# Time mixer of a hybrid decoder block: low-rank products and the three sums by ones as f32r products of split operands, in new instruction orders

## The reference, cut to what matters

```python
r, k, v, wl, al, gl = jnp.split(pf, cuts, axis=-1)          # 3 x 2048, 96, 96, 256
decay = jnp.exp(-DECAY_SCALE * jax.nn.sigmoid(w0 + jnp.tanh(wl) @ w_w2))
a = jax.nn.sigmoid(a0 + al @ w_a2)
g = jax.nn.sigmoid(gl) @ w_g2
kk = heads(k * k_k); kk = kk / jnp.maximum(jnp.linalg.norm(kk, axis=-1, keepdims=True), 1e-12)
k = k * (1.0 + (a - 1.0) * k_a)
y = rwkv7_scan(r_h, w_h, k_h, v_h, kk, a_h)                 # state S (64 x 64) per head, token after token
y = ((y - ym) * lax.rsqrt(yv + GN_EPS)) * gn_g + gn_b       # mean and variance over a head
bonus = jnp.sum(r_h * k_h * r_k, axis=-1, keepdims=True) * v_h
y = (y + bonus) * g
```

## Time and profile before

| what | value |
|---|---|
| median of the runs | 2427.96 us |
| the profiled execution | 2426.78 us, its span 2424.9 us |
| busy over the span | TensorE 2151.6 us (89%), VectorE 1532.0 (63%), ScalarE 676.7 (28%), GpSimd 668.7 (28%) |
| granted TensorE clock | 0.989 of full speed on the mean |
| software DMA queue (expert rows) | 537.01 MB, 52.7% of the 16 engines' span |
| VectorE, `w_half_rest` L192 | 224 instructions, 1218 ns each |
| ScalarE, `w_half_high` L171 | 224 instructions, 1051 ns each |

### The profile page before, as it was taken

The page is one execution under the profiler, slowest core; times in us unless marked ns, Lnnn a source line. Parts: engine busy times, 40 slices in busy tenths (PEclk is TensorE's granted clock), DMA queues, the critical chain, the costliest instruction groups (busy, mean ns, idle before and its releaser), DMA issues.

```text
span 2424.9 us, 37735 instructions
## 1 busy us (share of the span) xinstructions
PE 2151.6 (89%) x15287; PEld 1506.1 (62%) x15287; DVE 1532.0 (63%) x2592; ACT 676.7 (28%) x1353; POOL 668.7 (28%) x538
## 2 busy tenths in 40 slices
PE   7999999999999999998988988978887787777776
PEld 6999999999899999886544444433332233222222
DVE  7778888888765545558765577667445544444445
ACT  4555555555344444433111111111111000000000
POOL 1000000000000000004554555555455545444542
PEclk9999999999999999999999999999999999999999
DMA  5433333333366666677999999999999999999997
GB/s 201 131 105 101 104 89 96 102 89 100 106 188 192 186 185 188 198 249 276 416 416 424 421 426 427 427 426 427 427 427 427 426 427 427 428 427 427 427 427 289
DMA packets 346272, 708.19 MB, mean 292 GB/s; under 512 B 13834, under 2 KB 270434, under 8 KB 279778
## 3 DMA queue, kind: packets, MB, share of 16 engines
q0 software_dynamic: 74176, 537.01, 52.7%
q1 hardware_dynamic: 271684, 168.55, 23.5%
q10 hardware_dynamic: 240, 0.22, 0.0%
HBM read 703.63 MB, written 2.10 MB: 291 GB/s over the span
## 4 chain that ended last, share of the span: by engine, by line
DMA 33%; PE 15%; DVE 2%; issue 2%; POOL 1%; DVEq 1%; ACT 0%; POOLq 0%; ACTq 0%
DMA down_rows<-in_v_table,experts 25%; DMA up_rows<-in_u_table,experts 8%; PE bank L1782 8%; PE project L1782 4%; PE bank L1698 2%; POOL down_rows L1686 1%; DVE up_rows L1898 0%; PE bank L1740 0%; PE bank L1746 0%; PE bank L1725 0%; ACT diagonal L1842 0%; DVE one_hot L1348 0%; PE bank L1714 0%; DVE expert_sides L1354 0%; PE bank L1708 0%
## 5 line engine op out<-in xcount | busy, mean ns | idle before, releaser
L1898 DVE CUSTOM_DVE_ANT_0 up_rows<-up_rows,h 128x2048 f32<-128x2048 f32 x256 | 585.1, 2291 | 525.8 <-DMA up_rows<-in_u_table,experts 525.8
L1782 PE MATMUL bank<-down_rows,diagonal 128*128 128x512 f32 x1520 | 709.3, 603 | 144.5 <-DMA down_rows<-in_v_table,experts 112.0
L1782 PEld LDWEIGHTS bank<-down_rows,diagonal 128*128 128x128 f32 x1520 | 281.3, 191 | 554.4 <-issue 310.5
L1680 POOL DMA_INDIRECT up_rows<-in_u_table,experts x256 | 291.4, 1138 | 1159.2 <-POOLq L1366 1048.1
L1686 POOL DMA_INDIRECT down_rows<-in_v_table,experts x256 | 369.0, 1442 | 524.2 <-PE bank L1782 510.6
L192 DVE TENSOR_TENSOR w_half_rest<-w_half,w_half_high 128x1024 fp32r<-128x1024 f32 x224 | 271.3, 1218 | 160.1 <-ACT w_half_high L171 159.9
L207 PE MATMUL project<-hT_high,w_half_high 128*128 128x272 f32 (+1 forms) x1152 | 351.2, 305 | 0.4 <-PEq L214 0.3
L207 PE MATMUL project<-hT,w_half_high 128*128 128x272 f32 (+1 forms) x1152 | 329.3, 286 | 0.0
L207 PE MATMUL project<-hT_high,w_half_rest 128*128 128x272 f32 (+1 forms) x1152 | 328.8, 285 | 0.0
L1782 PE MATMUL project<-down_rows,diagonal 128*128 128x512 f32 x512 | 259.1, 630 | 71.2 <-DMA down_rows<-in_v_table,experts 65.8
L171 ACT CAST w_half_high<-w_half 128x1024 fp32r<-128x1024 f32 x224 | 234.8, 1051 | 205.4 <-PE merge_ps L207 121.0
(11 more groups left out here) (376 smaller groups left out, 3035.3 us busy)
## 6 DMA issues: line engine op xcount, KB each, us to landing
w_half<-in_w_in SPq DMA_DIRECT2D x176, 512.0 KB, 4.0
w_half<-in_w_branch_a SPq DMA_DIRECT2D x32, 512.0 KB, 3.7
out_w<-in_w_out SPq DMA_DIRECT2D x16, 1024.0 KB, 6.3
query_w<-in_w_q_peer SPq DMA_DIRECT2D x10, 1024.0 KB, 30.4
w_half<-in_w_branch_b SPq DMA_DIRECT2D x16, 512.0 KB, 3.7
out_w<-in_w_q_peer SPq DMA_DIRECT2D x6, 1024.0 KB
up_rows<-in_u_table,experts POOLq DMA_INDIRECT x256, 21.1
down_rows<-in_v_table,experts POOLq DMA_INDIRECT x256
```

The lines of the kernel that those rows point to most:

```text
L1680: pool.indirect_dma_start(ur[n % RU], None, w["u_table"][0], bass.IndirectOffsetOnAxis(ap=k.idx[:, t, h, j:j + 1], axis=0)).then_inc(s_u[n ...
L1782: mm = nc.tensor.matmul(acc[t][c][:], dg[n % RD][:], vr[n % RV][:, quarter(c)], start=(n == 0), stop=(n == last(t, c)), skip_group_check=True)
L1898: v.tensor_tensor_reduce(ur[n % RU], ur[n % RU], k.h[:, n // (HEADS * TOPK), :], 1.0, 0.0, ALU.mult, ALU.add, dots[:, n:n + 1]).then_inc(s ...
```

## The change

- The low-rank weights of a pair (four parts of 128 columns) go into one tile `w2` of 128x512, split by ScalarE (rounding) and VectorE (rest) in a new unit `lr`; the low-rank inputs are split once, at pair 0. Decay, rate and gate products then are three f32r products each (two times three for the gate).
- The squares of kk, the squares of y and r·k·r_k are split too: the squares are written twice by ScalarE, once rounded; r·k is rounded by ScalarE in a new unit `rq`. VectorE makes the rests in new units `nq`, `rq`, `gq`. The ones are exact in f32r, so each sum is two f32r products.
- k's rate factor (`k_scale`) moves from VectorE to ScalarE, behind the tanh of the rate.
- The three lists are new. SyncE loads a pair's low-rank weights when the split of the pair before has been made.
- The new tiles lie over tiles that are not yet in use (parts of `ya_high`, `ya_rest`, `pool_in`) or over the tile that they are made from.

```diff
 PE_ORDER = (
-    ("t", 1, 2), ("rb", 0, 2), ("u", 0, 3), ("lw", 0, 1), ("f", 10, 0), ("s", 0, 3), ("Z", 1, 2), ("r", 1, 3), ("la", 0, 1),
-    ("f", 3, 0), ("T", 1, 2), ("u", 1, 3), ("lg", 0, 1), ("f", 3, 0), ("s", 1, 3), ("r", 2, 3), ("T", 2, 2), ("u", 2, 3),
-    ("nm", 0, 1), ("f", 6, 0), ("s", 2, 3), ("r", 3, 3), ("T", 3, 2), ("u", 3, 3), ("f", 8, 0), ("s", 3, 3), ("r", 4, 3),
-    ("T", 4, 2), ("u", 4, 3), ("bo", 0, 1), ("f", 8, 0), ("s", 4, 3), ("Z", 5, 2), ("t", 0, 1), ("gv", 0, 3), ("f", 10, 0),
-    ("T", 5, 2), ("gr", 0, 1), ("r", 0, 2),
+    ("gr", 0, 2), ("t", 1, 2), ("u", 0, 3), ("f", 3, 0), ("lw", 0, 1), ("f", 2, 0), ("s", 0, 3), ("Z", 1, 2), ("rb", 0, 2),
+    ("r", 1, 3), ("f", 2, 0), ("la", 0, 1), ("f", 2, 0), ("lg", 0, 1), ("f", 6, 0), ("u", 1, 3), ("T", 1, 2), ("f", 3, 0),
+    ("s", 1, 3), ("r", 2, 3), ("T", 2, 2), ("u", 2, 3), ("f", 3, 0), ("s", 2, 3), ("r", 3, 3), ("T", 3, 2), ("u", 3, 3),
+    ("f", 2, 0), ("nm", 0, 1), ("f", 3, 0), ("s", 3, 3), ("r", 4, 3), ("T", 4, 2), ("f", 6, 0), ("bo", 0, 1), ("f", 5, 0),
+    ("Z", 5, 2), ("u", 4, 3), ("t", 0, 1), ("s", 4, 3), ("f", 4, 0), ("gv", 0, 3), ("f", 7, 0), ("r", 0, 2), ("T", 5, 2),
 )
 ACT_ORDER = (
-    ("sq", 0, 1), ("ge", 0, 4), ("lg", 0, 1), ("r", 2, 3), ("kn", 0, 1), ("e", 0, 0), ("ex", 0, 1), ("split", 4, 0),
-    ("u", 2, 3), ("nm", 0, 1), ("r", 3, 3), ("u", 3, 3), ("r", 4, 3), ("split", 5, 0), ("split", 0, -1), ("e", 1, 0),
-    ("u", 4, 3), ("yc", 0, 3), ("yf", 0, 2), ("gv", 0, 3), ("split", 1, -1), ("t", 0, 1), ("t", 1, 1), ("r", 0, 2), ("e", 2, 0),
-    ("u", 0, 2), ("lo", 0, 1), ("split", 2, -1), ("lw", 0, 0), ("la", 0, 0), ("r", 1, 2), ("ab", 0, 0), ("split", 3, -1),
-    ("u", 1, 2),
+    ("u", 0, 3), ("lo", 0, 2), ("lw", 0, 1), ("split", 2, 0), ("la", 0, 1), ("r", 1, 3), ("kn", 0, 1), ("split", 3, 0),
+    ("u", 1, 3), ("ex", 0, 1), ("r", 2, 3), ("e", 0, 0), ("rq", 0, 1), ("ge", 0, 4), ("u", 2, 3), ("sq", 0, 1), ("split", 4, 0),
+    ("r", 3, 3), ("u", 3, 3), ("lg", 0, 1), ("nm", 0, 1), ("ab", 0, 1), ("split", 5, 0), ("e", 1, 0), ("split", 0, -1),
+    ("yf", 0, 2), ("r", 4, 3), ("u", 4, 3), ("lr", 0, 0), ("yc", 0, 3), ("gv", 0, 3), ("r", 0, 2), ("e", 2, 0), ("t", 0, 1),
+    ("split", 1, -1), ("t", 1, 1),
 )
 DVE_ORDER = (
-    ("ge", 0, 4), ("split", 2, 0), ("go", 0, 4), ("s", 0, 3), ("e", 2, 1), ("rb", 0, 2), ("Z", 1, 2), ("r", 1, 3), ("la", 0, 1),
-    ("T", 1, 2), ("gy", 0, 4), ("s", 1, 3), ("cv", 0, 0), ("lk", 0, 1), ("split", 3, 0), ("T", 2, 2), ("r", 2, 3), ("s", 2, 3),
-    ("e", 0, 0), ("r", 3, 3), ("ks", 0, 1), ("T", 3, 2), ("split", 4, 0), ("s", 3, 3), ("nr", 0, 1), ("T", 4, 2), ("bo", 0, 1),
-    ("kb", 0, 1), ("rs", 0, 1), ("split", 5, 0), ("split", 0, -1), ("e", 1, 0), ("Z", 5, 2), ("split", 1, -1), ("T", 5, 2),
-    ("gr", 0, 1), ("Z", 0, 1), ("gm", 0, 1),
+    ("split", 5, 1), ("gq", 0, 4), ("split", 0, 0), ("lr", 0, 1), ("Z", 5, 3), ("ge", 0, 4), ("T", 5, 3), ("gr", 0, 2),
+    ("Z", 0, 2), ("split", 1, 0), ("gm", 0, 2), ("rs", 0, 2), ("s", 0, 3), ("Z", 1, 2), ("cv", 0, 0), ("rb", 0, 2),
+    ("la", 0, 1), ("e", 2, 1), ("split", 2, 0), ("go", 0, 4), ("r", 1, 3), ("lk", 0, 1), ("T", 1, 2), ("s", 1, 3),
+    ("split", 3, 0), ("T", 2, 2), ("r", 2, 3), ("s", 2, 3), ("gy", 0, 4), ("nq", 0, 1), ("split", 4, 0), ("r", 3, 3),
+    ("ks", 0, 1), ("T", 3, 2), ("s", 3, 3), ("e", 0, 0), ("rq", 0, 1), ("nr", 0, 1), ("T", 4, 2), ("bo", 0, 1), ("kb", 0, 1),
+    ("e", 1, 0),
 )
...
@block.sync
+                if b == 0:
+                    sp.wait_ge(q["zero"], n_zero)
-                wait(sp, q["lora_mm"], b * 3)
+                wait(sp, q["w2_split"], b)
...
@block.tensor
+            def low_rank(i, n, out, t0, start=True, stop=True):
+                return product(nc, out, [x[0:n, i, :] for x in (w2_high, w2_rest)], [x[0:n, i, t0:T] for x in (lora_high, lora_rest)], start, stop)
+            def by_ones(out, high, rest):
+                nc.tensor.matmul(out, ones_r[:].bitcast(F32R), high.bitcast(F32R), start=True, stop=False)
+                return nc.tensor.matmul(out, ones_r[:].bitcast(F32R), rest.bitcast(F32R), start=False, stop=True)
             def lw(_, p, par):
-                wait(pe, q["lora_w"], p * 48 + 48)
+                wait(pe, q["w2_split"], p + 1)
...
-                nc.tensor.matmul(low[:, 0:T], ww2[:], k.lora[0:DECAY_LORA, 0, :], start=True, stop=True).then_inc(q["lora_mm"], 1)
+                low_rank(0, DECAY_LORA, low[:, 0:T], 0).then_inc(q["lora_mm"], 1)
...
             def nm(_, p, par):
-                nc.tensor.matmul(low[:, 0:T], ones, sq[:, real], start=True, stop=True).then_inc(q["norm"], 1)
+                by_ones(low[:, 0:T], sq_high[:], sq_rest[:]).then_inc(q["norm"], 1)
...
@block.scalar
             def sq_(_, p, par):
+                nc.scalar.activation(sq_high[:].bitcast(F32R), kx[par][:, real], ACT.Square, scale=cur[par][:, V_KK:V_KK + 1])
+                nc.scalar.activation(sq[:], kx[par][:, real], ACT.Square, scale=cur[par][:, V_KK:V_KK + 1]).then_inc(q["ksq"], 1)
+            def lr(_, p, par):
+                if p == 0:
+                    for i, (_, c) in enumerate(k.lora_tiles):
+                        nc.scalar.copy(lora_high[0:c, i, :].bitcast(F32R), k.lora[0:c, i, :]).then_inc(q["lora_high"], 1)
+                wait(act, q["lora_mm"], p * 3)
+                wait(act, q["lora_w"], p * 48 + 48)
+                nc.scalar.copy(w2_high.bitcast(F32R), w2[:]).then_inc(q["w2_high"], 1)
+            def rq(_, p, par):
+                wait(act, q["bonus"], p)
+                wait(act, q["rk"], p + 1)
+                nc.scalar.copy(rk_high.bitcast(F32R), rk[:]).then_inc(q["rkhigh"], 1)
             def la(_, p, par):
...
+                act.wait_ge(q["sig"], p * 3 + 2)
+                nc.scalar.activation(t1[:, real], am[:, real], ACT.Identity, scale=cur[par][:, V_KAH:V_KAH + 1],
+                                     bias=cur[par][:, V_KAC:V_KAC + 1]).then_inc(q["kscale"], 1)
             def y(_, p, par):
+                nc.scalar.activation(ysq_high.bitcast(F32R), y_ps, ACT.Square)
...
@block.vector
             def la(_, p, par):
-                wait(dve, q["sig"], p * 3 + 2)
-                n.tensor_scalar(t1[:, real], am[:, real], cur[par][:, V_KAH:V_KAH + 1], cur[par][:, V_KAC:V_KAC + 1], ALU.mult, ALU.add)
             def lk(_, p, par):
+                wait(dve, q["kscale"], p + 1)
+            def lr(_, p, par):
+                if p == 0:
+                    n.tensor_copy(ones_r[:].bitcast(F32R), ones).then_inc(q["ones"], 1)
+                    for i, (_, c) in enumerate(k.lora_tiles):
+                        dve.wait_ge(q["lora_high"], i + 1)
+                        rest_bits(n, lora_rest[0:c, i, :], k.lora[0:c, i, :], lora_high[0:c, i, :])
+                wait(dve, q["w2_high"], p + 1)
+                rest_bits(n, w2_rest, w2[:], w2_high).then_inc(q["w2_split"], 1)
+            def nq(_, p, par):
+                rest_bits(n, sq_rest[:], sq[:], sq_high[:]).then_inc(q["ksplit"], 1)
+            def rq(_, p, par):
+                rest_bits(n, rk_rest[:], rk[:], rk_high).then_inc(q["rksplit"], 1)
+            def gq(_, p, par):
+                rest_bits(n, ysq_rest[:], ysq[:], ysq_high).then_inc(q["sqsplit"], 1)
```

More of the change, by code:

```diff
@@ L688, in lg @@
                 for j in range(2):
-                    mm = nc.tensor.matmul(low[:, 0:SEQ], wg2[:, j, :], k.lora[:, 2 + j, META:T], start=(j == 0), stop=(j == 1))
+                    mm = low_rank(2 + j, P, low[:, 0:SEQ], META, j == 0, j == 1)
                 mm.then_inc(q["lora_mm"], 1)
@@ L693, in nm @@
                 wait(pe, q["sig"], p * 3 + 3)
-                wait(pe, q["ksq"], p + 1)
-                nc.tensor.matmul(low[:, 0:T], ones, sq[:, real], start=True, stop=True).then_inc(q["norm"], 1)
+                wait(pe, q["ones"], 1)
+                wait(pe, q["ksplit"], p + 1)
+                by_ones(low[:, 0:T], sq_high[:], sq_rest[:]).then_inc(q["norm"], 1)
             def bo(_, p, par):
                 wait(pe, q["nroot"], p + 1)
-                wait(pe, q["rk"], p + 1)
-                nc.tensor.matmul(low[:, 0:SEQ], ones, rk[:, CH:TP], start=True, stop=True).then_inc(q["bonus"], 1)
+                wait(pe, q["rksplit"], p + 1)
+                by_ones(low[:, 0:SEQ], rk_high, rk_rest[:]).then_inc(q["bonus"], 1)
             def gr(_, p, par):
@@ L798, in gv @@
             def gv(_, p, par):
-                wait(pe, q["sqr"], p + 1)
-                nc.tensor.matmul(var_ps, ones, ysq[:], start=True, stop=True).then_inc(q["var"], 1)
+                wait(pe, q["sqsplit"], p + 1)
+                by_ones(var_ps, ysq_high, ysq_rest[:]).then_inc(q["var"], 1)
             schedule(PE_ORDER, {"f": f, "lw": lw, "la": la, "lg": lg, "nm": nm, "bo": bo, "gr": gr, "rb": rb, "t": t,
```

47 lines of the change are left out of this document (34 added, 13 removed).

## The result

The changed kernel takes 2431.48 us (median of 21 runs, 2430.43 to 2432.45), the kernel before 2428.53 us (21 runs, 2425.43 to 2430.24): ratio 1.0015, interval 1.001 to 1.0021. That is slower by 0.15%, with 2418.5 us forecast and a range that ended at 2430. The profiled execution took 2431.89 us (span 2430.0), 5.1 us more in span than the one of before, which is one of its kernel's faster runs (2426.78 us); by medians the difference is 2.95 us.

The account below looks back on a forecast made before the run. TensorE's instruction stream was taken to bound the mixer. 16 x (0.93 − 0.3) = 10.1 us, less 0.6 us for the fill, gave a gain of 9.5 us: 2418.5 us, range 2412 to 2430 us.

Parts of the forecast that it names:

- The bound and the stages: TensorE's instruction stream bounds the mixer; merge and expert stage stay untouched, so time saved in the mixer shortens the span.
- TensorE's saving of 0.93 us: Mixer, per pair: f32r products replacing f32 ones save TensorE 0.93 us, 14.9 us over 16 pairs.
- VectorE's load: Mixer, per pair: net +1.2 to +1.3 us; VectorE's turn without waits becomes 32.8 to 33.2 us and still fits.
- The rival that makes VectorE's total the bound: VectorE keeps its old waits: 36.8 us per pair, +24 us, 2452 us; in full or in part, chance 0.11.
- The state chain: TensorE's chunk product, VectorE's new S, TensorE's next chunk: stalls counted at 0.10 us per pair.
- The two intervals: Between successive state products: VectorE 3.16 and 4.21 us against TensorE 3.13 and 4.14, so behind by 0.03 and 0.07.
- Steady lateness: At the states VectorE trails by 0.03 and 0.07 us without meeting TensorE's signal anew, which would add 0.18 to each.
- ScalarE's places: Tanh before the gate product, and work between two copies on the way to the fourth chunk: 0.1 us per pair together.
- the end of the pair: Transposes of a pair's A, B and V follow its B product closely: 0.1 us per pair.
- Fill and tail: Filling the pipeline costs 0.6 us once; the tail, 590 to 720 us, counts 0 but may give or take 2.
- The second: Rival: the chain costs 0.5 us per pair, ScalarE and the pair's end 0.3; 2426.5 us, chance 0.22.
- the signs that the prediction gave for being wrong: Period over 35.1 us; TensorE waits over 10 us for S, rhs or B_st; merge starting earlier but ending unchanged.

Follow-up runs that it names:

- undo_nm: The changed kernel with the sum of k's squares again one f32 product and VectorE's rest of them (nq) gone: 2432.30 us, ratio 1.0020.
- orders_only: The kernel before with the three new lists alone, f32 products and k's rate factor on VectorE: 2447.55 us, ratio 1.0081.
- gq_later: The changed kernel with the rest of y's squares (gq) moved behind the next weight split in VectorE's list: 2431.55 us, ratio 1.0018.
- undo_var: The changed kernel with the variance sum again one f32 product and no rest of y's squares (gq): 2434.76 us, ratio 1.0032.
- go_early: The changed kernel with gq behind the next weight split and y's scaling and gating (go) moved ahead of T5 in VectorE's list: 2430.49 us, ratio 1.0005.
- gy_early: go_early with VectorE's rest of ya (gy) moved ahead of T1 and ScalarE's rounding of ya earlier: 2424.92 us, ratio 0.9989.
- run tail: The changed kernel with the last pair's pooling window ahead of VectorE's wait for y's squares instead of behind it: 2429.98 us, ratio 1.0012.

## Why the prediction was wrong

**The bound and the stages.** Right. The merge and the experts kept their length (1738.4 to 1738.3 us). In the other kernels it lies between 1737.4 and 1740.3 us, 1741.3 in undo_nm, so what the mixer gains or loses comes out at the end, to one or two microseconds of a single execution.

**TensorE's saving of 0.93 us.** Right in size: 0.92 with equal lists (orders_only to after), 0.34 for the low-rank products (priced 0.33), 0.25 to 0.27 for one sum (0.19 to 0.21). Against the kernel before only 0.77 arrive, since the new list has the gate product 0.15 us late in every pair. "It drops out" was said of the switches between wide and small products, and it held.

**VectorE's load.** Right: turn without waits forecast at 32.8 to 33.2 us. VectorE's waits in the steady part now add to 31 us, 2.2 per pair, which leaves 33.2. The rival that makes VectorE's total the bound was rightly thought unlikely: gq_later and undo_var exclude it.

**The state chain: the step that failed.** The prediction put 0.10 us per pair there; the S stall rose by 0.78, from 0.31 to 1.09, and took five sixths of the 0.93. Two things were wrong.
- It compared the engines only from s1 to s2 and s2 to s3. Nothing was added up from T5 to T1, where the new list has `gm`, `rs`, the scan, `go` and two splits. VectorE comes late to s1 already, by 0.33 (0.42 less the 0.09 that always stands there). go_early takes exactly this stall away and leaves the two others.
- The two intervals were 0.1 and 0.2 short: 356.00 − 352.76 = 3.24 and 360.39 − 356.00 = 4.39, where 3.16 and 4.21 stood. What the sums left out is a call of `nc.vector.drain()` that the kernel makes ahead of S and of its decay (units `s` and `r`). Behind such a call an instruction starts 0.07 to 0.10 us after the end of the one ahead, whether it reads its result (S at 356.00, with S_decayed over at 355.92) or not (S_decayed at 358.20, behind a split that is over at 358.10). Without the call it starts some 0.08 us ahead of that end (the split at 352.96, with S over at 353.04). In the first interval I took the whole bracket of 0.18 at 354.66 for waiting, and the drain is in it (S_decayed is over at 354.48). In the second I took the step from Z_st to a split, 357.13 to 357.47, 0.34 us; in the new order S stands behind Z_st with a drain between them, 359.88 to 360.39, 0.51 us. By the Trainium skill (VectorE: DVE Perf Modes, The DRAIN you can't avoid) the next operation does not start until the pipeline is empty, and one that is not held starts earlier. The trace has both: the late start where the program's own drain stands, the early one where VectorE has neither a drain nor a wait ahead.

The two rows of the kernel before that these readings use and that the earlier trace rows does not have:

```profile
354.23 0.25 DVE L1061 TENSOR_SCALAR S_decayed<-S,chunk_decay 128x64 f32<-128x64 f32 x1
...
357.13 0.42 DVE L1031 TENSOR_TENSOR Z_st<-X_blocks,constants 128x256 f32<-128x256 f32 x1
```

"Steady lateness" was also the wrong picture: a late S delays TensorE, which delays T5's product, and VectorE's next stretch starts from it. The lateness closes a loop and is paid again in each turn: without 0.33 of it (go_early) the period is shorter by 0.23, without 0.63 of it (gy_early) by 0.53.

**ScalarE's places, the end of the pair.** Priced at 0.1 each. The prediction said of the gate product that the tanh "fits by some 0.05 us". It does not, and costs 0.15 us per pair: a second, smaller step that was wrong, shown by the rows and by the 0.15 of orders_only; no run moves the gate product back. No wait of TensorE stands at the other place, and for the end of the pair it lists 0.2 us for B_st over 14 pairs.

**Fill and tail.** Priced 0.6 and 0. The first decay product is 2.2 us later (72.18 against 69.98), but 0.9 of that stands there before the mixer begins: the first wide product is at 52.28 against 51.39, and in the other kernels, whose front stage is the same, it lies anywhere from 51.3 to 52.6, so this is scatter of single executions. From the first wide product to the first decay product it is 19.9 against 18.6 us: 1.3 us for the fill, of which orders_only shows 1.1 as the order's, which has three projection steps ahead of the decay product. The tail cost 2.6 us, `gq`'s wait with the window behind it, and the run tail takes all of it away. The bound of ±2 for the tail was just too narrow; the code would have shown that a VectorE wait on ScalarE stood ahead of the last pair's window.

**The rivals.** The second had the right mechanism, "VectorE meets TensorE anew", and too small a price for the chain: 0.5 where 0.78 came. Of its 0.3 for ScalarE and the end of the pair, 0.15 came, and it had no tail. With 0.78 + 0.15 in place of its terms the gain per pair is 0.93 − 0.93 = 0, which is what the period shows, and fill and tail then make the sign. Of the signs that the prediction gave for being wrong, the period over 35.1 us came; TensorE's listed wait for S stayed at 6.4 of the 10 us, with 12.0 at its weight loads.
